# Shared rows in a table of their own, closing blocks that write one table, and a tail that reads one table

## The chip, the cores and the metric

The kernel runs on one core of a Trainium2 chip. The metric is the device time of one execution in microseconds (us): the median of 3 runs before the change is 1509.52 us (1507.58 to 1512.52). All data are fp32.

## The reference, cut to what matters

One layer over 1024 prompt tokens and 8 sample tokens, D = 1024. First a mixer (projection, convolution, retention, output projection), which leaves `x` (called x2 in the kernel) and the normed rows `h`. Then the part that the change touches:

```python
h = rmsnorm(x, g_ffn) * (1 + sc_f) + sh_f
x = x + gt_f * moe(h, ...)             # gt_f: one row for the prompt
# moe: 64 experts of width 256, top 6 per token
#   routed[t] = sum over 6 chosen experts of w * ((silu(h@w1[e]) * (h@w3[e])) @ w2[e])
#   shared    = (silu(h@ws1) * (h@ws3)) @ ws2
#   return routed + shared
y = x * rsqrt(mean(x*x) + eps) * g_final   # final RMSNorm
```

## The kernel before, in words

Up to about 712 us the mixer, the router and the sorting of tokens run. Then comes the **block stage**. Its unit is a block of 128 token slots; there are NX = 57 of them. The slots are dealt out in quarters of 32, so that a block serves one to three experts, in an order written out by a table (`GROUPS`, `LINE`, `QUARTERS`, lines 40 to 95). 64 experts x 3 MB of weights pass through five buffers, the ring (`SLOT`); expert s may be loaded into its slot when the block `FREE[s]` has finished with the former tenant: w1 and w3 after that block's up-product (`h_done`), w2 after its down-product (`y_done`). SP issues all these loads in order (`load_in_line`, lines 605 to 620, with L558 and L562 as the DMA lines).

Per block x:
- PE runs `up(x)` (L1017, 8 matmuls of 128x512 for a block with one expert), then `down(x-1)` (L1033, 4 matmuls), then `hidden_trans(x)` (L1023). `await_weights(x)` stands before `up`.
- ACT takes the SiLU (L1329), DVE the product (L1753), the scaling of the output by the routing weight (`blk_y`, L1764), the copy of the transposed hidden rows (L1757) and the transposes of gathered rows (`xpose`, L1744).
- POOL gathers block x+3 (L2005, 4 indirect DMAs) and then adds the scaled rows of block x into a DRAM table (`scatter`, L2014, an accumulating indirect DMA). A scatter waits for the one before it. Two tables lie behind each other in `acc_rows`; an expert's place in the line decides which of them it writes (even or odd), so both are complete only after the last scatters.

The shared expert is worked off beside this: `sh_down(n)` (L776) runs for 9 tiles of tokens, one in every fourth block from block 8 on (`SHARED_AT`). DVE multiplies each by gt_f (L1731), adds x2 (L1733), and ACT's DMA queue stores the sum back over x2 (`store_shared`, L1278) after it has loaded the old rows (`load_x2`, L1274).

**The tail** begins when both chains of scatters have landed (SP waits at lines 655 to 657). SP has loaded g_final and the 8 tiles of x2 beforehand (L646, L648). It now loads 3 small sample pieces and, alternately, 8 tiles of each table (L663, L664). PE adds the two tables by products with the identity (L1126; tile 0 is added on DVE, L1931), DVE multiplies by gt_f (L1935) and adds x2 (L1938), ACT squares and takes the root (L1350, L1353), DVE scales (`finish`, L1919, L1920), SP stores (L667).

Where the order of work is set: each engine runs its own written list; only semaphores join them. SP's list counts most here, since all big loads are in it one behind the other.

Of the kernel before, what the change touches and what calls it, by code (L numbers as in the profile page):

```python
# [20 lines left out]
P = 128  # L21
# [52 lines left out]
GROUPS = even_order(groups())  # L74
# [6 lines left out]
NU = len(QUARTERS) // 4  # L81
assert NU % 2 == 1 and all(len({x for x, _ in QUARTERS[4 * u:4 * u + 4]}) < 3 for u in range(NU))
# [19 lines left out]
SHARED_AT = tuple(8 + 4 * n for n in range(NT))  # L102
# [27 lines left out]
def build(nc, t, out):  # L130
    with ExitStack() as ctx:
# [3 lines left out]
        def sem(name):  # L135
# [32 lines left out]
        x3_ready, fin_ssq, fin_std, dve_step, pool_step = (  # L168
            sem(n) for n in "x3_ready fin_ssq fin_std dve_step pool_step".split())
# [5 lines left out]
        acc_in = [win_in[0], win_in[1]] + [win_in[2 + i // 2] for i in range(TP - 2)]  # L175
        acc_there = [16 + 32, 16 + 32] + [16 + 64] * (TP - 2)
# [16 lines left out]
        sh_rows_s = scratch("sh_rows_s", (NS, D))  # L193
# [44 lines left out]
        acc_t = [W[:, WE + D * i:WE + D * i + D] for i in range(TP)]  # L238
        acc_s = W[:, WE + TP * D:WE + TP * D + SW]
        odd_t = [W[:, WE + (TP + 1 + i) * D:WE + (TP + 1 + i) * D + D] for i in range(TP)]  # L240
        odd_s = W[:, WE + TP * D + SW:WE + TP * D + 2 * SW]
        sh_s = W[:, WE + TP * D + 2 * SW:WE + TP * D + 3 * SW]
# [95 lines left out]
        sh_x2 = (gt_m, gret[:, :, :].rearrange("p v n -> p (v n)"))  # L338
# [26 lines left out]
        x2_t += [mods[:, 2, :], mods[:, 3, :]]  # L365
        x2_s, gt_s, g_s = (gret[:, 0, SW * x:SW * x + SW] for x in range(3))
# [39 lines left out]
        def _(sp):  # L406
# [217 lines left out]

            rounds = sp.value_load(rounds_i, min_val=0, max_val=ROUNDS)
# [17 lines left out]
            sp.wait_ge(x2_in, 16)  # L643
            for n in range(2):
                sp.wait_ge(sh_stored[n], 16 * ((NT + 1 - n) // 2))
            sp.dma_start(g_fin, everywhere(t["g_final"].rearrange("(a n) -> a n", a=1))).then_inc(x2_in, 16)  # L646
            for i in range(TP):
                sp.dma_start(x2_t[i], x2_rows[P * i:P * i + P, :]).then_inc(x2_in, 16)  # L648
# [27 lines left out]
        def _(pe):  # L676
# [418 lines left out]
            for x in range(1, NX):  # L1095
                await_weights(x)
                up(x, parts_of(x), x % 2)
                if x in SHARED_AT:
                    sh_down(SHARED_AT.index(x))
# [1028 lines left out]
```

## Time and profile before

| | |
|---|---|
| median of 3 runs | 1509.52 us |
| the profiled execution | 1507.41 us, its span 1505.6 us |
| mixer and routing | 0 to 712 us of the span |
| block stage | first up-product 746.55 us, last evacuation 1447.79 us |
| last scatters | issued at 1435.67, 1445.46 and 1451.77 us, the last landed by 1458.17 us |
| tail | from 1458.17 us to the end |
| PE busy over the span | 1357.6 us (90%) |
| bytes moved | 370.74 MB, mean 246 GB/s |

The times of instructions below count from the start of the span. Between the end of the last instruction and the device time of the same execution lie 1.8 us.

### The profile page before, as it was taken

The page shows a single profiled execution, that of the slowest core. Times are in us where ns is not written, and L with a number is a line of the kernel's source. Part 1 is how long each engine was busy: PE and PEld are TensorE (multiplying, and loading weights), DVE is VectorE, ACT ScalarE, POOL GpSimd, SP SyncE. Part 2 cuts the span into 40 slices and gives each one's busy share as a digit, 9 for nine tenths or more (in the row PEclk, how much of TensorE's full clock was granted, in tenths as well). Part 3 has the DMA queues.
Part 4 walks back from the last instruction along what each step waited for, and adds up shares of the span by engine and source line. Part 5 has one row for each costly group of instructions (what it writes and reads, how often), then busy time and mean ns, then how long its engine had stood idle before and what let it go on. Part 6 is the DMA issues. An engine that isn't in the chain of part 4 may idle for free.

```text
span 1505.6 us, 17406 instructions
## 1 busy us (share of the span) xinstructions
PE 1357.6 (90%) x5860; PEld 616.6 (41%) x5860; DVE 823.9 (55%) x2088; ACT 207.0 (14%) x347; POOL 438.8 (29%) x379
## 2 busy tenths in 40 slices
PE   4889999999989999899699989989989999879947
PEld 2344454545545554455343433433333333323313
DVE  1048686988988899987233333332433343332327
ACT  1121223223131313232000000000000000000003
POOL 0000120212111112224334434444444444453410
PEclk9899999999999999999899999999999999999978
DMA  9988212121121001812999999999999999999976
GB/s 322 334 316 306 107 56 87 42 101 59 70 90 40 33 28 51 251 38 74 357 383 379 366 372 341 392 379 334 377 365 374 372 374 365 346 377 353 371 206 262
DMA packets 96810, 370.74 MB, mean 246 GB/s; under 512 B 18493, under 2 KB 32801, under 8 KB 71967
## 3 DMA queue, kind: packets, MB, share of 16 engines
q1 hardware_dynamic: 73463, 310.40, 53.4%
q0 software_dynamic: 20944, 50.89, 13.1%
q10 hardware_dynamic: 2320, 8.42, 1.4%
q8 instruction: 43, 0.70, 0.2%
q14 instruction: 40, 0.33, 0.1%
HBM read 326.03 MB, written 64.30 MB: 259 GB/s over the span
## 4 chain that ended last, share of the span: by engine, by line
PE 31%; DMA 12%; issue 5%; DVE 2%; POOL 1%; SPq 0%; ACT 0%; POOLq 0%; ACTq 0%
PE U L1017 19%; PE R L1033 9%; DMA acc_rows<-W,kT 5%; DMA acc_rows<-xr,kT 5%; PE X L776 2%; DMA W<-h_rows,q_r 1%; PE T L1023 1%; DMA front<-h_rows,q_r 1%; DVE W L1920 1%; DVE W L1938 1%; DVE W L1935 1%; PE R L1126 0%; DMA W<-acc_rows 0%; POOL W L2005 0%; POOL front L2005 0%
## 5 line engine op out<-in xcount | busy, mean ns | idle before, releaser
L729 PE MATMUL U<-W,front 128*128 128x512 f32 x768 | 343.7, 602 | 1.2 <-issue 1.2
L1435 DVE SCALAR_TENSOR_TENSOR cv<-win,cw,cv 128x128 f32<-128x128 f32 x960 | 256.6, 346 | 1.4
L1017 PE MATMUL U<-W,cat 128*32 128x512 f32 (+2 forms) x848 | 211.9, 625 | 24.4 <-issue 15.9
L1017 PE MATMUL U<-W,front 128*32 128x512 f32 (+2 forms) x1056 | 202.7, 611 | 17.4 <-issue 17.4
L729 PEld LDWEIGHTS U<-W,front 128*128 128x128 f32 x768 | 145.0, 194 | 168.6 <-issue 168.6
L1033 PE MATMUL R<-W,glu 128*32 128x512 f32 (+2 forms) x952 | 207.9, 596 | 1.3 <-DVE glu L1757 1.3
L1744 DVE STREAM_TRANSPOSE front<-front 128x1024 f32<-128x1024 f32 x28 | 57.3, 2045 | 147.9 <-DMA front<-h_rows,q_r 147.9
L1017 PEld LDWEIGHTS U<-W,cat 128*32 128x32 f32 (+2 forms) x848 | 78.2, 147 | 137.2 <-issue 136.1
L2005 POOL DMA_INDIRECT W<-h_rows,q_r x116 | 117.2, 1010 | 48.6 <-issue 34.8
L1033 PEld LDWEIGHTS R<-W,glu 128*32 128x32 f32 (+2 forms) x952 | 71.2, 134 | 131.5 <-issue 130.0
L1744 DVE STREAM_TRANSPOSE cat<-W 128x1024 f32<-128x1024 f32 x29 | 59.2, 2041 | 118.8 <-DMA W<-h_rows,q_r 107.6
L1017 PEld LDWEIGHTS U<-W,front 128*32 128x32 f32 (+2 forms) x1056 | 70.4, 131 | 128.9 <-issue 127.3
L2005 POOL DMA_INDIRECT front<-h_rows,q_r x112 | 112.9, 1008 | 34.2 <-issue 34.2
L823 PE MATMUL R<-W,cat 128*128 128x512 f32 x256 | 114.7, 606 | 1.7 <-ACT cat L1258 1.7
L1329 ACT ACTIVATE sg<-U 128x256 f32<-128x256 f32 x57 | 21.8, 383 | 682.6 <-PE U L1017 682.6
L1969 POOL DMA_INDIRECT list_tab<-list_val,list_row x54 | 54.2, 1004 | 187.6 <-DVE list_row L1529 141.7
L1960 POOL TENSOR_TENSOR o_t<-o_t,gret 128x512 f32<-128x512 f32 x8 | 10.1, 1264 | 297.5 <-DVE o_t L1596 278.6
L2014 POOL DMA_INDIRECT acc_rows<-xr,kT x29 | 46.6, 1607 | 169.0 <-DMA acc_rows<-W,kT 116.3
L2014 POOL DMA_INDIRECT acc_rows<-W,kT x28 | 44.7, 1598 | 157.0 <-DMA acc_rows<-xr,kT 85.8
L823 PEld LDWEIGHTS R<-W,cat 128*128 128x128 f32 x256 | 49.1, 194 | 61.0 <-issue 59.1
L1764 DVE TENSOR_SCALAR W<-R,kT 128x1024 f32<-128x1024 f32 x28 | 35.9, 1283 | 63.2 <-PE R L1033 63.0
L1753 DVE TENSOR_TENSOR sg<-U,sg 128x256 f32<-128x256 f32 x57 | 22.8, 400 | 83.6 <-ACT sg L1329 83.6
(371 smaller groups left out, 1216.5 us busy)
## 6 DMA issues: line engine op xcount, KB each, us to landing
W<-in_w SPq DMA_DIRECT2D x192, 1024.0 KB, 18.4
W<-in_w_ada SPq DMA_DIRECT2D x24, 1024.0 KB, 8.6
W<-in_w_in SPq DMA_DIRECT2D x6, 2048.0 KB, 19.9
W<-acc_rows SPq DMA_DIRECT2D x16, 512.0 KB, 9.7
front<-in_x_prompt SPq DMA_DIRECT2D x8, 512.0 KB
W<-in_w_out SPq DMA_DIRECT2D x1, 4096.0 KB, 17.8
xr<-in_x_prompt SPq DMA_DIRECT2D x8, 512.0 KB, 4.2
x_rows<-xr SPq DMA_DIRECT2D x8, 512.0 KB, 3.3
```

The lines of the kernel that those rows point to most:

```text
L729: last = mm(U[BANK[g]][:, :], hT[:, k, :], w_in[:, k, 512 * g:512 * g + 512], start=k == 0, stop=k == KT - 1)
L776: last = mm(X[0:rows, 512 * half:512 * half + 512], sh_hidT[g][f][:, at:at + rows], sh_w2[:, f, 512 * half:512 * half + 512], start=f == 0 ...
L823: last = mm(R[:, 512 * n:512 * n + 512], cat[:, k, :], w_out[:, k, 512 * n:512 * n + 512], start=start and k == ks[0], stop=stop and k == ...
L1017: last = mm(U[1][cols, :], xgT[z][:, k, cols], w13[:, :, k, :], start=k == 0, stop=k == KT - 1)
L1033: last = mm(R[cols, 512 * half:512 * half + 512], hidT[:, f, cols], weights[:, at:at + 512], start=f == 0, stop=f == FT - 1)
L1435: ins = v.scalar_tensor_tensor(cv[:, c, :], win[:, c, w:w + P], cw[:, c, w:w + 1], cv[:, c, :], ALU.mult, ALU.add)
L1744: v.transpose(xgT[z][:, :, :].rearrange("p k (q t) -> p k q t", q=4), xgs[r].rearrange("p (q t k) -> p k q t", q=4, k=KT)).then_inc(xgT_re ...
L1753: v.tensor_tensor(hid, U[1][:, DE:2 * DE], hsil, ALU.mult).then_inc(hid_ready, 1)
L1764: v.tensor_scalar(y_sbs[x % 2], R[:, :], slot_w[:, x:x + 1], None, ALU.mult).then_inc(y_evac, 1)
L1969: pool.indirect_dma_start(list_tab, bass.IndirectOffsetOnAxis(ap=list_row[0:rows, k:k + 1], axis=0), list_val[0:rows, k, :], None, bounds_ ...
L2005: pool.indirect_dma_start(xgs[x % 2][:, QW * q:QW * q + QW], None, h2_quarters, bass.IndirectOffsetOnAxis(ap=at[:, q, :], axis=0), bounds_ ...
L2014: pool.indirect_dma_start(acc_rows, bass.IndirectOffsetOnAxis(ap=at, axis=0), y_sbs[x % 2], None, bounds_check=2 * TABLE - 1, oob_is_err=F ...
```

## The change

Four things are changed, in one step.

1. **Shared rows.** `shared_out(n)` on ACT copies the product of `sh_down(n)` from PSUM and stores it to a DRAM table `shared_rows`. DVE's `sh_add` and the loads of x2 within the stage are gone; x2 stays as it was. Tiles 0 to 2 are done before the first block, the other six in every sixth block from block 8 on.
2. **The order of blocks.** Three groups with one expert and one block each (`CLOSING`) are taken out of the evenly spread order and put at the end. Their experts write the first table, so that the second is complete after block `ODD_LAST` = 53.
3. **Base rows.** For each of 8 tiles PE adds the shared rows and the odd table's rows (`base(i)`), and DVE multiplies by gt_f and adds x2 (`base_add(i)`), in place in `x2_t[i]`. `base(0)` stands between `up(56)` and `down(55)`, `base(1)` between `hidden_trans(56)` and `down(56)`, the others behind `down(56)`.
4. **Tail.** 8 tiles of one table are loaded. DVE multiplies by gt_f (`gate`), PE adds the base rows by the identity into PSUM, ACT and DVE read the sum from PSUM.

How the table of blocks changes (block: the experts by place in line whose weights it is the first to need; then, in brackets, the `FREE` block of each):

```
before   49: 55 56 [44 46]   50: 57 [46]   52: 58 59 [48 48]   53: 60 [49]   55: 61 [51]   56: 62 63 [52 52]
after    46: 54 55 [41 43]   47: 56 [43]   48: 57 [45]   49: 58 [46]   51: 59 [46]   53: 60 [48]   54: 61 [48]   55: 62 [50]   56: 63 [53]
```

The core of the diff:

```diff
+CLOSING = [x for x in MADE if len(x) == 1 and units_of(x) == 1][-3:]
+GROUPS = even_order([x for x in MADE if x not in CLOSING]) + CLOSING
+TABLE_OF = tuple(i % 2 for group in GROUPS for i in range(len(group)))
+END = [max(LAST[s] for s in range(NE) if SLOT[s] == r) for r in range(RING + 1)]   # 56 55 53 54 45
-SHARED_AT = tuple(8 + 4 * n for n in range(NT))
+SHARED_AT = (-1, -1, -1) + tuple(8 + 6 * n for n in range(NT - 3))
+        odd_in = [c_in] * 6 + [modv_in] * 2
+        odd_there = [48 + 96] * 6 + [80 + 32] * 2
+        shared_in = [sconv_in] * 2 + [disp_in] * 6
+        shared_there = [48 + 32] * 2 + [32 + 96] * 6
@@ sync, behind the last load_in_line
+            sp.wait_ge(y_done, END[RING] + 1)
+            for i in range(TP):
+                sp.dma_start(x2_t[i], x2_rows[P * i:P * i + P, :]).then_inc(x2_in, 16)
+            sp.dma_start(g_fin, ...).then_inc(x2_in, 16)
+            for i in range(2):
+                load_shared_rows(i)
+            sp.wait_ge(y_done, END[2] + 1)
+            sp.wait_ge(scattered[ODD_LAST % 2], 16 * (ODD_LAST // 2 + 1))
+            for i in range(6):
+                load_odd(i)
+            sp.wait_ge(xgT_ready, NX)
+            load_odd(6)
+            sp.wait_ge(h_done, NX - 1)
+            load_odd(7)
+            sp.wait_ge(y_done, END[3] + 1)
+            for i in range(2, TP):
+                load_shared_rows(i)
...
             for i in range(TP):
                 sp.dma_start(acc_t[i], ...).then_inc(acc_in[i], 16)
-                sp.dma_start(odd_t[i], ...).then_inc(acc_in[i], 16)
@@ tensor
+            sh_down(0)                       # ahead of spread_lists(); 1 and 2 ahead of up(0)
+            def base(i):
+                pe.wait_ge(shared_in[i], shared_there[i])
+                pe.wait_ge(odd_in[i], odd_there[i])
+                pe.wait_ge(base_ready, floor(i - 1))
+                for half in range(2):
+                    cols = slice(512 * half, 512 * half + 512)
+                    mm(base_banks[i % 2][half], ident[:, :], shared_t[i][:, cols], start=True, stop=False)
+                    last = mm(base_banks[i % 2][half], ident[:, :], odd_t[i][:, cols], start=False, stop=True)
+                last.then_inc(base_posed, 1)
-            for i in range(1, TP):
-                pe.wait_ge(acc_in[i], acc_there[i])
-                pe.wait_ge(gated, floor(i - 1))
+            for i in range(TP):
+                pe.wait_ge(gated, i + 1)
+                pe.wait_ge(base_ready, TP if i == 1 else i + 1)
+                pe.wait_ge(fin_ready, floor(i - 1))
                 for half in (slice(0, 512), slice(512, 1024)):
...
+                    mm((R, X)[i % 2][:, half], ident[:, :], acc_t[i][:, half], start=True, stop=False)
+                    last = mm((R, X)[i % 2][:, half], ident[:, :], x2_t[i][:, half], start=False, stop=True)
@@ scalar
+            def shared_out(n):
+                act.wait_ge(sh_downs, n + 1)
+                act.wait_ge(sh_stored[n % 2], 16 * (n // 2))
+                nc.scalar.activation(sh_y[n % 2][0:sh_rows(n), :], X[0:sh_rows(n), :], ACT.Copy).then_inc(sh_copied, 1)
+                act.wait_ge(sh_copied, n + 1)
+                act.dma_start(shared_rows[...], sh_y[n % 2][...]).then_inc(sh_stored[n % 2], 16)
@@ vector
+            def base_add(i):                 # even tiles: the same in four halves
+                    link(v.tensor_tensor(X[:, :], X[:, :], gt_f, ALU.mult))
+                    v.tensor_tensor(x2_t[i], X[:, :], x2_t[i], ALU.add).then_inc(base_ready, 1)
+            base_add(0)
             blk_y(NX - 1)
+            for i in range(1, TP):
+                base_add(i)
+            def gate(i):
+                dve.wait_ge(acc_in[i], acc_there[i])
+                v.tensor_tensor(acc_t[i], acc_t[i], gt_f, ALU.mult).then_inc(gated, 1)
+            for i in range(2, TP):
+                gate(i)
+                finish(i - 2)
```

How PE's list ends. Before, from the transpose of block 55 on (`sg` holds the hidden rows, `glu` the transposed ones, `U` and `R` are PSUM banks):

```order
L1023 MATMUL T<-ident,sg 128x128
L1017 MATMUL U<-W,cat 64x512 [waits xgT_ready,ring_in3,ring_in0]
L1017 MATMUL U<-W,cat 64x512 x15
L1033 MATMUL R<-W,glu 64x512 [waits y_evac,hidT_ready]
L1033 MATMUL R<-W,glu 64x512 x7
L1023 MATMUL T<-ident,sg 128x128 [waits hid_ready]
L1023 MATMUL T<-ident,sg 128x128
L1033 MATMUL R<-W,glu 64x512 [waits y_evac,hidT_ready]
L1033 MATMUL R<-W,glu 64x512 x7
```

After, the same place, from the down-product of block 55 on (`mods` and `W` hold the shared and the odd rows):

```order
L1134 MATMUL R<-W,ident 128x512
L1064 MATMUL R<-W,glu 128x512 [waits y_evac,hidT_ready]
L1064 MATMUL R<-W,glu 128x512 x3
L1054 MATMUL T<-ident,sg 128x128 [waits hid_ready]
L1054 MATMUL T<-ident,sg 128x128
L1133 MATMUL X<-mods,ident 128x512 [waits base_ready,c_in,sconv_in]
L1134 MATMUL X<-W,ident 128x512
L1133 MATMUL X<-mods,ident 128x512
L1134 MATMUL X<-W,ident 128x512
L1064 MATMUL R<-W,glu 128x512 [waits y_evac,hidT_ready]
L1064 MATMUL R<-W,glu 128x512 x3
L1133 MATMUL U<-W,ident 128x512 [waits base_ready,c_in,disp_in]
```

The first row is the last of `base(0)`'s four matmuls, which stand ahead of the down-product of block 55; `base(1)`'s four stand between the transpose and the down-product of block 56, and `base(2)` begins behind it.

SP's list behind the last expert's weights, before (`in_w` are expert weights, `x_rows` is x2):

```order
L558 DMA W<-in_w 128x2048 x2
L562 DMA W<-in_w 128x2048 [waits y_done]
L625 TENSOR_LOAD k_r
L646 DMA mods<-in_g_final 128x1024 [waits sh_stored1,sh_stored0,x2_in]
L648 DMA W<-x_rows 128x1024 x6
L648 DMA mods<-x_rows 128x1024 x2
```

and after:

```order
L568 DMA W<-in_w 128x2048 x2
L572 DMA W<-in_w 128x2048 [waits y_done]
L640 DMA W<-x_rows 128x1024 [waits sh_stored1,y_done,sh_stored0,x2_in]
L640 DMA W<-x_rows 128x1024 x5
L641 DMA mods<-in_g_final 128x1024
L644 DMA mods<-shared_rows 128x1024 x2
L647 DMA W<-acc_rows 128x1024 [waits scattered1,y_done]
L647 DMA W<-acc_rows 128x1024 x5
L647 DMA front<-acc_rows 128x1024 [waits xgT_ready]
L647 DMA front<-acc_rows 128x1024 [waits h_done]
L644 DMA W<-shared_rows 128x1024 [waits y_done]
L644 DMA W<-shared_rows 128x1024 x5
```

Between the last weights and the tail, 24 tiles of 512 KB (x2, odd and shared rows) stand where 8 stood; the odd table's eight were in the tail before, and no list read the shared rows of the prompt.

## Rows read from the trace of the kernel before

**Rows 1.** Stages: us, busy time by engine, PEclk, DMA share, GB/s.
```profile
core 0: us, PE busy (x) PEld busy (x) DVE busy (x) ACT busy (x) POOL busy (x), PEclk, DMA share, GB/s
800.00:900.00 100.00, 94.53 (x422) 36.94 (x423) 33.90 (x34) 3.06 (x8) 45.12 (x40) 0.98 1.01 373
...
1440.00:1460.00 20.00, 6.45 (x30) 1.95 (x26) 2.90 (x3) 0.00 (x0) 3.10 (x2) 0.82 0.45 78
1460.00:1480.00 20.00, 12.57 (x24) 5.60 (x25) 10.42 (x13) 4.52 (x9) 0.00 (x0) 0.67 1.00 389
```

**Rows 2.** PE's longest wait in the block stage: waits from 720 to 1440 us.
```profile
PE U L1017 <- issue: 33.3, 6, 8.1
```

**Rows 3.** The chain of waits, 1340 to 1365 us: start, us, what.
```profile
1345.54 8.10 issue
1353.64 8.85 PE U L1017 x32
```

**Rows 4.** The chain of waits over the stage: one `sh_down`.
```profile
946.87 3.43 PE X L776 x8
```

**Rows 5.** ACT's SiLU of blocks 50 and 51: the pace of the last eight blocks.
```profile
1373.27 0.38 ACT L1329 ACTIVATE sg<-U 128x256 f32<-128x256 f32 x1 [10.36 <-PE U L1017]
1384.16 0.38 ACT L1329 ACTIVATE sg<-U 128x256 f32<-128x256 f32 x1 [10.50 <-PE U L1017]
...
1438.98 0.38 ACT L1329 ACTIVATE sg<-U 128x256 f32<-128x256 f32 x1 [11.20 <-PE U L1017]
```

**Rows 6.** DMA queues, 1200 to 1300 us (packets, MB, share): q1 SP's, q10 ACT's.
```profile
q1 hardware_dynamic: 3765, 27.40, 67.6%
...
q10 hardware_dynamic: 160, 0.56, 1.4%
```

**Rows 7.** DMA queues and landing times, 1416 to 1440 us.
```profile
q1 hardware_dynamic: 1912, 7.20, 75.2%
...
W<-x_rows SPq DMA_DIRECT2D x6, 512.0 KB, 16.8
```

**Rows 8.** PE ahead of the first block, 718 to 757 us.
```profile
728.17 0.64 PE L1051 MATMUL U<-ident,k_d 128*32 128x128 f32 x2 [5.79 <-DMA k_d<-list_tab,v_t]
...
734.29 3.72 PE L765 MATMUL T<-front,W 128*128 128x264 f32 x16
746.55 8.65 PE L1017 MATMUL U<-W,cat 128*128 128x512 f32 x16 [8.54 <-DVE cat L1744]
```

**Rows 9.** POOL's scatter of block 54 and DVE's evacuation of block 56.
```profile
1435.67 1.58 POOL L2014 DMA_INDIRECT acc_rows<-xr,kT  x1 [8.46 <-DMA acc_rows<-W,kT]
...
1447.79 1.28 DVE L1764 TENSOR_SCALAR xr<-R,kT 128x1024 f32<-128x1024 f32 x1 [3.76 <-PE R L1033]
```

**Rows 10.** DMA landing times in us, 1450 to 1460 us.
```profile
W<-acc_rows SPq DMA_DIRECT2D x2, 512.0 KB, 4.4
W<-acc_rows SPq DMA_DIRECT2D x2, 32.0 KB, 1.7
```

**Rows 11.** The tail: PE's identity sums, ACT, DVE and SP, by start.
```profile
1458.17 0.35 SPq L659 DMA_DIRECT2D W<-acc_rows  x1
...
1467.43 6.58 PE L1126 MATMUL R<-W,ident 128*128 128x512 f32 x8 [19.69 <-DMA W<-acc_rows]
...
1487.81 3.60 PE L1126 MATMUL X<-W,ident 128*128 128x512 f32 x8
...
1491.24 3.60 PE L1126 MATMUL R<-W,ident 128*128 128x512 f32 x8
...
1496.78 1.22 DVE L1935 TENSOR_TENSOR W<-R,mods 128x1024 f32<-128x1024 f32 x1
1498.03 1.23 DVE L1938 TENSOR_TENSOR W<-W,mods 128x1024 f32<-128x1024 f32 x1
1499.35 1.06 ACT L1350 ACTIVATE sig<-W 128x1024 bf16<-128x1024 f32 x1 [2.31 <-DVE W L1938]
...
1501.06 1.28 DVE L1920 SCALAR_TENSOR_TENSOR W<-W,sm,mods 128x1024 f32<-128x1024 f32 x1
```

More of the change, by code:

```diff
@@ L237, in build @@
         x2_t = [shw[:, D * i:D * i + D] for i in range(6)]
[L238 to L242, printed above, removed]
+        odd_t = [W[:, WE + D * i:WE + D * i + D] for i in range(6)]
+        acc_t = [W[:, 4 * WE + D * i:4 * WE + D * i + D] for i in range(6)] + [W[:, 2 * WE + D * i:2 * WE + D * i + D] for i in range(2)]
+        acc_s, odd_s, sh_s = (W[:, 2 * WE + 2 * D + SW * i:2 * WE + 2 * D + SW * i + SW] for i in range(3))
+        shared_t = [W[:, 3 * WE + D * i:3 * WE + D * i + D] for i in range(6)]
         ident = sb("ident", [P, P])
@@ L364, in build @@
         gt_f, g_fin = mods[:, 0, :], mods[:, 1, :]
-        x2_t += [mods[:, 2, :], mods[:, 3, :]]
-        x2_s, gt_s, g_s = (gret[:, 0, SW * x:SW * x + SW] for x in range(3))
+        x2_t += sh_y
+        odd_t += [x_t[:, :], front[:, D:2 * D]]
+        shared_t = [mods[:, 3, :], mods[:, 4, :]] + shared_t
+        x2_s, gt_s, g_s = (maskT[:, x, 0:SW] for x in range(1, 4))
         same_row = maskT[:, 0, :]
@@ L641, in _ @@
                         load_expert(e, 0)
[L643 to L648, printed above, removed]
-            sp.dma_start(same_row, t["same_row"]).then_inc(sample_in, 16)
-            sp.dma_start(x2_s, in_pieces(x2_rows[SEQ:TOKENS, :])).then_inc(sample_in, 16)
-            for b in range(NS):
-                rows = slice(b * P // NS, (b + 1) * P // NS)
-                sp.dma_start(gt_s[rows], in_pieces(mod_rows[1 + b:2 + b, 5 * D:6 * D])).then_inc(sample_in, 16)
-                sp.dma_start(g_s[rows], t["g_final"].rearrange("(c n) -> c n", n=SW)).then_inc(sample_in, 16)
             sp.wait_ge(scattered[0], 16 * EVEN + 16 * NE * rounds)
@@ L1073, in _ @@
             sh_up_part(2, 1, 1)
+            sh_down(1)
+            sh_down(2)
             def parts_of(x):
@@ L1099, in _ @@
                     sh_down(SHARED_AT.index(x))
+                if x == NX - 1:
+                    base(0)
                 down(x - 1, parts_of(x - 1))
                 hidden_trans(x)
+                if x == NX - 1:
+                    base(1)
                 if x == 3:
@@ L1105, in _ @@
             down(NX - 1, parts_of(NX - 1))
+            for i in range(2, TP):
+                base(i)
             ring_0 = [(0, 4, ring[0])]
@@ L1318, in _ @@
             score(TP - 1)
-            for g in (1, 2):
-                sh_silu_part(g, 0)
-                sh_silu_part(g, 1)
-            act.wait_ge(x2_stored, 16 * TP)
-            for n in range(2):
-                load_x2(n)
+            sh_silu_part(1, 0)
+            sh_silu_part(1, 1)
+            sh_silu_part(2, 0)
+            shared_out(0)
+            sh_silu_part(2, 1)
+            shared_out(1)
+            shared_out(2)
             def blk_silu(n):
@@ L1927, in _ @@
             v.tensor_tensor(acc_s, acc_s, x2_s, ALU.add).then_inc(x3s_ready, 1)
-            for i in range(TP):
-                if i == 0:
-                    dve.wait_ge(acc_in[i], acc_there[i])
-                    link(v.tensor_tensor(acc_t[i], acc_t[i], odd_t[i], ALU.add))
-                    ins = v.tensor_tensor(acc_t[i], acc_t[i], gt_f, ALU.mult)
-                else:
-                    dve.wait_ge(sum_done, i)
-                    ins = v.tensor_tensor(acc_t[i], (X, R)[i % 2][:, :], gt_f, ALU.mult)
-                ins.then_inc(gated, 1)
-                dve.wait_ge(gated, i + 1)
-                v.tensor_tensor(acc_t[i], acc_t[i], x2_t[i], ALU.add).then_inc(x3_ready, 1)
-                if i > 0:
-                    finish(i - 1)
+            for i in range(2, TP):
+                gate(i)
+                finish(i - 2)
+            finish(TP - 2)
             finish(TP - 1)
```

85 lines of the change are left out of this document (44 added, 41 removed).

## The prediction, written before the changed kernel was run

> **What bounds the kernel now.** I read the stages first, then PE's waits, then the chain of waits, the DMA queues, and last the tail in order of time. The stages show the two halves of the question. In the block stage the DMA engines are busy all the time (share 1.01) while PE is busy 94.5%; in the tail the DMA share falls and TensorE's clock with it [rows 1]. PE's waits in the block stage are 6 in number and 33.3 us in sum, all at an up-product and with "issue" as the releaser [rows 2], which the kernel's code explains: `await_weights` stands there. The chain shows the last of them: PE waits 8.10 us for the weights of block 49, and then runs the rest of the stage without one [rows 3]. So up to block 49 the stage goes at the pace at which weights arrive, and from there at PE's pace, 10.9 us for a block [rows 5]. After it come the last scatters; the one of block 54 begins at 1435.67 us, that of 56 waits for its evacuation at 1447.79 us and for 55's landing [rows 9]; the tail starts at 1458.17 us [rows 11]. In the tail PE's sum of two tiles takes 3.60 us by its row and 3.43 from one start to the next (1487.81 to 1491.24), the first one 6.58 us at the lower of the two clocks, and DVE spends 1.22 + 1.23 + 1.28 = 3.7 us per tile and a short reciprocal [rows 11]: DVE bounds the tail.
>
> **The block stage.** The weights' bytes are the same, 3.15 MB for each expert. What changes is what goes beside them and by when they are needed.
> - *Bytes gone.* In the stage, six loads of x2 and eight stores of full tiles (0.52 MB each) become five stores: 9 x 0.524 = 4.7 MB less. SP's and ACT's queues together moved 27.40 + 0.56 = 28.0 MB in 100 us [rows 6], SP's alone 7.20 MB in 24 us [rows 7], so 0.28 to 0.30 MB per us; I take 0.29. That is 16.2 us of weights' time. The three early stores take the place of two early loads of x2, 0.52 MB more at a time when the queues are full: +1.3 us.
> - *Need moved forward.* By the tables of blocks, block 49 waited for the 57th expert of the line (place 56). In the new order the last place where the demand is as dense is block 46, which needs the 56th (place 55): one expert fewer, 3.15 / 0.29 = 10.8 us earlier. These weights then land at 1353.6 - 16.2 + 1.3 - 10.8 = 1327.9 us. But behind block 46 stand 11 blocks, not 8. Before, from the end of the wait to the evacuation of block 56 it was 1447.8 - 1353.6 = 94.2 us for 8 blocks [rows 3, 9]; three more at 10.9 us [rows 5] make 126.9. The evacuation of block 56 would thus come at 1454.8 us, **7 us later** than now, although 4.7 MB fewer are moved. The closing blocks need a whole expert each, but their loads are issued three blocks ahead and I see no wait there.
> - *What is free.* `sh_down` costs PE 3.43 us [rows 4]. Three of them leave the stage, which gives nothing while PE waits for weights anyway, and stand before it: number 0 fits in the wait of 5.79 us at 728.17, numbers 1 and 2 (6.9 us and a copy of about 1.1 between, by ACT's row of 1.06 for the same elements [rows 11]) in the 8.54 us ahead of the first up-product [rows 8]. If that cover failed, it would cost 2 to 3 us, which the weights' pace would take up. DVE loses 8 x 2.4 us of work beside PE, ACT gains 9 copies of about a microsecond: neither bounds the stage.
>
> **The wait of `base(0)`.** It stands ahead of `down(55)`, so behind it on PE are the down-products of blocks 55 and 56, and behind those two scatters. Its semaphore counts all six first tiles of the odd table. Those are issued when block 53's scatter has landed, 1435.67 us before [rows 9], 1442.7 with the 7 us. In SP's queue they stand behind 1.05 MB of weights, 4.19 of x2, 0.52 of g_final and 1.05 of shared rows, all issued from the end of `down(53)` on (about 1427): 6.81 MB at the 7.20 MB in 24 us of such a stretch [rows 7], 0.30 MB per us, is 22.7 us, up to 1449.7. The six tiles, 3.15 MB at the tail's 389 GB/s [rows 1], since POOL has one scatter left to move, take 8.1 us, and the landing about 1.7 [rows 10]: 1459.5 us. `up(56)` ends at 1438.98 + 7.1 = 1446.1 [rows 5]. **PE waits 13.4 us.** From both sides: 0 if the odd tiles came without a queue before them, 20 if POOL's traffic ran beside them all the time. PE then begins at the lower clock. After 19.69 us of idling, the mean granted clock being 0.82 in its first 20 us and 0.67 in the next [rows 1], the same four matmuls took 6.58 us [rows 11]; I take 6.6 (3.4 if the clock stayed).
>
> The Trainium skill (DMA: Bandwidth & Descriptors, "Queues, rings and completion order") says that each DMA engine consumes a queue's descriptors in ring order. The trace fits: the x2 tiles, issued behind weights, landed 16.8 us after issue [rows 7]. By that page's limit of about 358 GB/s from HBM (section "Specifications") the six tiles would take 8.8 us, 0.7 more; the tail's 389 GB/s [rows 1] is above it, and the measurement decides.
>
> **PE's work behind the blocks.** `base(i)` is the same work as the tail's sums: 4 matmuls of 128x512 with the identity. `base(0)` 6.6 and `base(1)` 3.4 us delay `down(56)`: evacuation at 1454.8 + 13.4 + 6.6 + 3.4 = 1478.2. `base(2)` to `base(7)`: 6 x 3.43 = 20.6, to 1498.8. DVE's `base_add` (2.45 us for an odd tile by the rows of 1.22 and 1.23, four halves of 0.7 for an even one by estimate from these) keeps up with 3.43; only the last is added: 2.45. Then `gate(0)`, 1.23, which stands behind it on DVE: 1502.5. Block 56's scatter, issued about 1480, has landed by 1487 and the 8 tiles of 0.52 MB (10.8 us at 389 GB/s) by 1500: hidden.
>
> **The tail.** PE bounds it: 8 sums x 3.43 = 27.4 us, where 7 sums ran beside DVE before. A sum waits for the finish two tiles earlier; from SQUARE's start to the end of the scaling it is 1501.06 + 1.28 - 1499.35 = 2.99 us [rows 11], under 3.43. These two now read PSUM; an evacuation of that size from PSUM takes 1.28 [rows 9], the same as the scaling from SBUF, so I add nothing (between nothing and 0.4 per tile, which the gap to 3.43 covers). To 1529.9. Last square to scaling 3.0: 1532.9. From the last scaling to the span's end it was 1505.6 - 1502.3 = 3.3: **span 1536.2**, 30.6 more. The loads taken out of the tail (4.2 MB) give nothing, as DVE was its bound. The profiled execution took 1507.4 at a span of 1505.6; with the same 1.8 the new one takes 1538.0. The median lies 2.1 above the profiled run; I forecast 1540.
>
> **Rivals.**
> - *A: the odd tiles are in time and `base(0)` does not wait.* For it: 0.52 MB loads land in 4.4 us where the queue is empty [rows 10]. Against: 6.8 MB stand before them. Then 13.4 + 3.2 us fall away: 1536.2 - 16.6 = 1519.6 of span, 1523 as a median.
> - *B (the other side): the stage gets its 16 us.* If the last wait for weights stayed 8 blocks from the end, the freed bytes would bring the evacuation of block 56 to 1447.8 - 16.2 + 1.3 = 1432.9; and if `base(0)` doesn't wait either, the rest is 6.9 (two bases) + 20.6 + 2.45 + 1.23 + 27.4 + 6.3 = 64.9: span 1497.8, median 1502. It decides where the evacuation of block 56, without the bases, comes before 1505.6 - 64.9 = 1440.7, 7 us earlier than now. For it: PE's 33.3 us of waits are there to be won. Against: 11 blocks of PE's pace from block 46 on.
> - *C: the order costs the stage nothing (evacuation at 1447.8), but `base(0)` waits as forecast:* 1529 of span, 1533. Its result lies in the forecast's own spread.
> - *D: more waits.* The closing blocks take 3.15 MB in each 10.9 us, and block 56's w2 is issued only after `down(53)`; if it comes late, PE waits 3 to 10 us more at block 56 (the base tiles then come nearer to that, so about half is kept): 1543 to 1546.
>
> **How the numbers follow.** Forecast with C and D as its spread 0.76 (1530 to 1552), A 0.15, B 0.06, something else 0.03. The range that leaves out two in ten at most: 1518 to 1550. What a measurement of this kernel can tell from no change is 0.3%, 4.5 us. Slower by more: 0.90, within: 0.04, faster: 0.06.
>
> **What would show it.** In the new trace: the last "issue" wait of PE ahead of an up-product at block 46 (wrong if at 49 or later, then the stage's sum fails); a wait of 10 to 17 us at the first identity product with the odd rows as releaser, and that product at 6.6 us (wrong: A); six identity products without a gap behind the last down-product; tail products of 3.4 us in an unbroken row with DVE waiting for PE, and no row of tail loads in the chain. A span under 1515 would refute the sum as a whole.

## The result, and the profile after

The changed kernel takes 1547.83 us (median of 4 runs, 1545.36 to 1550.95) against 1510.05 us of the kernel before on the same chip: a ratio of 1.0245, 95% interval 1.0216 to 1.0275, 37.8 us slower. The forecast was 1540, in a range of 1518 to 1550. The profiled execution took 1545.5 us with a span of 1543.6.

The waits of PE from 720 us to the end (us in sum, times, longest) answer to [rows 2]:
```profile
PE U L1048 <- issue: 45.2, 8, 8.5
PE U L1133 <- issue: 14.2, 1, 14.2
PE R L1177 <- DVE W L1976: 7.8, 1, 7.8
```
The waits for weights grew from 33.3 to 45.2 us. Three more follow: 14.2 us ahead of the first identity product, and 7.8 us and, further on, 1.06 us in the tail, where PE stood idle for 19.69 us before [rows 11].

The chain of waits of the changed kernel (start, us, what) answers to [rows 3]:
```profile
1319.59 8.49 issue
1328.09 9.17 PE U L1048 x32
...
1434.37 18.62 DMA mods<-shared_rows
1452.99 7.76 issue
1460.75 2.05 PE U L1133 x2
...
1498.58 1.24 DVE X L1936
1505.05 1.24 DVE W L1976
...
1512.98 1.28 ACT L1402
```
The last wait for weights ends at 1328.09 us. Then nothing is late until the base tiles. The chain passes through the shared rows' loads, which land at 1452.99; the 7.76 us from there to 1460.75 have no releaser in this trace. The odd rows' loads are the ones behind them in SP's list, and a later kernel names them at the same product. Between the last `base_add` and the first gate the chain has a hole.

The stages, in the columns of [rows 1]:
```profile
1440.00:1460.00 20.00, 6.55 (x16) 2.61 (x14) 1.53 (x3) 0.39 (x1) 1.58 (x1) 0.79 1.03 386
1460.00:1480.00 20.00, 19.25 (x41) 8.70 (x42) 6.75 (x9) 0.00 (x0) 2.17 (x2) 0.86 0.63 209
1480.00:1500.00 20.00, 18.12 (x42) 7.52 (x40) 14.94 (x19) 0.00 (x0) 0.93 (x1) 1.00 0.72 235
1500.00:1520.00 20.00, 12.61 (x25) 5.42 (x26) 10.45 (x14) 4.46 (x9) 0.00 (x0) 0.83 0.09 38
```
From 1440 to 1460 us the DMA engines are full (1.03; before 0.45) and PE is idle for two thirds of the time. From 1500 to 1520 nothing is bound by DMA (0.09), and PE is busy for 12.61 us of 20 only.

The end in order of time, all engines, answers to [rows 5, 9, 11]:
```profile
1446.59 0.39 ACT L1382 ACTIVATE sg<-U 128x256 f32<-128x256 f32 x1 [10.14 <-PE U L1048]
1460.75 2.05 PE L1133 MATMUL U<-mods,ident 128*128 128x512 f32 x2 [14.20 <-issue]
1477.32 1.28 DVE L1801 TENSOR_SCALAR xr<-R,kT 128x1024 f32<-128x1024 f32 x1 [2.96 <-PE R L1064]
1499.85 1.22 DVE L1937 TENSOR_TENSOR gret<-X,gret 128x1024 f32<-128x1024 f32 x1
1505.05 2.36 DVE L1976 TENSOR_TENSOR W<-W,mods 128x1024 f32<-128x1024 f32 x2 [3.98 <-issue]
1506.33 2.08 PE L1177 MATMUL R<-W,ident 128*128 128x512 f32 x2 [7.79 <-DVE W L1976]
1512.98 1.28 ACT L1402 ACT_TABLE_LOAD   x1
1516.23 1.10 PE L1177 MATMUL R<-W,ident 128*128 128x512 f32 x2 [1.06 <-DVE W L1972]
1539.08 1.28 DVE L1972 SCALAR_TENSOR_TENSOR W<-X,sm,mods 128x1024 f32<-128x1024 f32 x1
```
Block 56 has its up-product at 1446.59 us but is evacuated at 1477.32, because PE stands before `base(0)`. The last `base_add` ends at 1501.07 and the first gate starts at 1505.05. For these 3.98 us DVE is idle, and the profile names no other engine or transfer that it waited for ("issue").

### The profile page after: what moved, and what is told of

Read it like the earlier page. It is cut to its first block, busy times and chain, and to the rows that moved or that the text cites. A ratio compares the mean times of both kernels' runs of the same rounds, so it can differ in the third digit from the quotient of the medians.

```text
span 1543.6 us, 17575 instructions
## 1 busy us (share of the span) xinstructions
PE 1398.4 (91%) x5932; PEld 634.2 (41%) x5932; DVE 814.2 (53%) x2086; ACT 216.6 (14%) x356; POOL 438.8 (28%) x379
## 4 chain that ended last, share of the span: by engine, by line
PE 48%; DVE 19%; DMA 16%; issue 9%; SPq 4%; ACT 2%; POOL 2%; DVEq 0%; POOLq 0%; ACTq 0%
PE U L1048 15%; DVE cv L1484 8%; PE R L1064 8%; PE U L760 7%; PE R L854 6%; DMA acc_rows<-W,kT 5%; DMA acc_rows<-xr,kT 4%; PE X L807 2%; DMA W<-h_rows,q_r 2%; SPq L448 2%; DMA W<-in_w_ada 2%; DMA front<-h_rows,q_r 1%; PE X L796 1%; DMA mods<-shared_rows 1%; PE R L724 1%
## 5 line engine op out<-in xcount | busy, mean ns | idle before, releaser
L2062 POOL DMA_INDIRECT acc_rows<-W,kT x28 | 44.7, 1598 | 189.6 <-DVE W L1801 119.1
```

Source lines behind the costliest of these rows:

```text
L2062: pool.indirect_dma_start(acc_rows, bass.IndirectOffsetOnAxis(ap=at, axis=0), y_sbs[x % 2], None, bounds_check=2 * TABLE - 1, oob_is_err=F ...
```

## The experiments

Each result stands beside the kernel before, run on the same chip. Two kernels, the first part of the change as a whole and the one with the loops moved, ran on another chip than the rest; the kernel before took 1511.02 us there and 1509.99 on the first. The ratios and their intervals are estimates from all the runs of both kernels, not quotients of the two medians. The experiments go from the block stage to the end.

### The order alone
```
--- the kernel before
-GROUPS = even_order(groups())
+MADE = groups()
+CLOSING = [x for x in MADE if len(x) == 1 and units_of(x) == 1][-3:]
+GROUPS = even_order([x for x in MADE if x not in CLOSING]) + CLOSING
```


> The kernel before with the changed order of blocks alone (closing groups at the end); tables, shared rows and tail as before. My theory: the last wait for weights moves from block 49 to about block 46, and 11 blocks at 10.9 us stand behind it instead of 8, less 10.8 us for one expert fewer: +22 us, 1532. Rival: PE's 33 us of waits are slack that the order only deals out anew: within 5 us of before, 1510.

Measured: 1529.75 us (1527.81 to 1530.74), ratio 1.0117 (1.0086 to 1.0147), 19.7 us slower. The theory holds (1532 forecast), and its rival (1510) falls: the evacuation of block 56 comes at 1469.42, 21.6 us later than before. PE's up-products that waited for weights, of this kernel, the fourth, sixth and last of eight:
```profile
996.19 8.43 PE L1019 MATMUL U<-W,front 128*32 128x512 f32 x64 [6.61 <-issue]
...
1141.78 9.02 PE L1019 MATMUL U<-W,cat 128*32 128x512 f32 x64 [11.73 <-issue]
...
1343.21 7.30 PE L1019 MATMUL U<-W,cat 128*64 128x512 f32 x24 [6.27 <-issue]
```
and the same three of the changed kernel:
```profile
988.23 8.41 PE L1048 MATMUL U<-W,front 128*32 128x512 f32 x64 [7.15 <-issue]
...
1127.23 8.88 PE L1048 MATMUL U<-W,cat 128*32 128x512 f32 x64 [8.32 <-issue]
...
1328.09 9.17 PE L1048 MATMUL U<-W,cat 128*64 128x512 f32 x32 [8.49 <-issue]
```
With the order alone the last wait ends at 1343.21, block 46, 10.4 us earlier than the 1353.6 of [rows 3], and three blocks more follow. That holds the prediction's second step. The first, the bytes, is the difference of the two fences: 8.0 us at the fourth wait, 14.6 at the sixth, 15.1 at the last (14.9 forecast, 16.2 less 1.3). This difference holds more than bytes: with them three `sh_down` left the stage, 10.3 us of PE's work, and no run takes the two apart in the new order.

### The bytes alone, in the old order
First without the loads of x2 in the stage:
```
--- the kernel before
-            for n in range(2):
-                load_x2(n)
...
-                    load_x2(n + 2)
...
-                v.tensor_tensor(sh_x2[n % 2], X[:, :], sh_x2[n % 2], ALU.add).then_inc(sh_copied, 1)
+                v.tensor_copy(sh_x2[n % 2], X[:, :]).then_inc(sh_copied, 1)
```


> The kernel before, but the eight loads of x2 in the block stage are left out, and the shared expert's rows are stored (as bytes, after the multiplication by gt_f) to a table that nobody reads; the shared part is missing in the output. Order and tail as before. My theory: the stage up to block 49 goes at the pace of bytes, 4.2 MB fewer at 0.29 MB per us are 14.5 us: 1495. Rival: the weights' landing is set by slots coming free, not by bytes: 1508 to 1510.

Measured: 1501.87 us (1496.32 to 1503.89), ratio 0.9929 (0.99 to 0.9958), 8.1 us faster: between the theory (1495) and its rival (1508 to 1510). Then the first part of the change as a whole, which keeps the output:
```
--- the kernel before
+SHARED_AT = (-1, -1, -1) + tuple(8 + 6 * n for n in range(NT - 3))
...
+            for i in range(TP):
+                if i >= 4:
+                    sp.wait_ge(base_ready, i - 3)
+                sp.dma_start(x2_t[i], x2_rows[P * i:P * i + P, :]).then_inc(ada_in[i % 4], 16)
...
+                    sp.dma_start(part, shared_rows[P * i:P * i + P, wide * z:wide * z + wide]).then_inc(stage_in[i % 4], 16)
...
+                    ins = v.tensor_tensor(part, part, gt_f[:, wide * z:wide * z + wide], ALU.mult)
...
+                    ins = v.tensor_tensor(to, part, to, ALU.add)
```


> Part 1 of the change alone, in the old order of blocks: shared rows stored plainly by ACT, tiles 0 to 2 ahead of the blocks. x2 and shared rows (not the odd table) are loaded behind the last weights through four staging buffers, DVE alone makes x2 + gt_f * shared (tile 0 in block 55, tile 1 in block 56, the others behind the last evacuation), no sum on PE but the old tail's. Theory 1: bytes and the three down-products that leave the stage both count, as between the run with the order alone and the changed kernel (last wait for weights ends at 1343.2 and 1328.1): here it ends at 1338.5 instead of 1353.6, the last evacuation at 1433; the extra loads beside the last scatters give back 3 to 8 us, so 1498 to 1502. Theory 2: only the loads' bytes count, 8 us as in the run without x2 loads: last wait ends at 1345, and with the same contention no gain at all, 1505 to 1510.

Measured: 1509.42 us (12 runs) against 1511.02, ratio 0.9986 (0.9967 to 1.0005): no difference. That is what theory 2 said (last wait ends at 1345, 1505 to 1510); theory 1 falls. The chain of waits of the kernel without the loads of x2:
```profile
1337.21 7.91 issue
1345.12 9.29 PE U L1018 x32
```
and of the one with the first part whole:
```profile
1336.87 8.00 issue
1344.87 9.36 PE U L1026 x32
```
Both end the last wait 8.5 to 8.8 us earlier than before, whether 4.2 MB or the whole first part's bytes are gone. By bytes at 0.29 MB per us it would have been 14.5 and about 15. One observation narrows the cause: the w2 of the expert at place 56 was issued 8.3 us earlier without the loads (1325.95 against 1334.27 us), and PE's wait ended about 19 us behind that issue in both. Ahead of it SP issued nothing for 13.3 us in either kernel (from 1320.92 before). So in the old order the last weights are held back by the slot that PE must free first, and not only by the bytes before them. Why the first part as a whole is worth 15.1 us in the new order and 8.8 in the old one stays open. PE stands idle for longer in the new order (51.8 us with the order alone against 33.3), so there is more to be won; that this is the reason isn't shown.

Part one gained 8.6 us up to the evacuation of block 56 (1439.23, [rows 9]: 1447.79) and ended where it began. POOL and SP of this kernel show where it went:
```profile
1448.04 2.48 POOL L2028 DMA_INDIRECT acc_rows<-xr,kT  x1 [8.75 <-DMA acc_rows<-W,kT]
...
1455.03 0.42 SPq L645 DMA_DIRECT2D maskT<-in_g_final  x1
...
1460.23 0.35 SPq L668 DMA_DIRECT2D W<-acc_rows  x1
```
From the last scatter to the tail's first load it is 12.2 us here, against 6.4 before (1451.77 to 1458.17). But only 7.4 of them are the scatter, which has landed at 1455.4. SP is what comes last: it issues its small loads until 1455.45, and for the next 4.8 us the trace shows no instruction of it. By the program these are its own reading of the number of extra rounds and its own empty loop over them. In the kernel before that loop stood ahead of the loads of g_final and x2, where SP shows a like gap (1411.88 to 1416.55) long before the tail. The change moved these loads ahead of the loop, and so the loop to the end. The same 4.8 us stand behind the small loads in five of the kernels below, however early the last scatter has landed.

### The base sums out of the way of the last blocks
```
--- the changed kernel
-                if x == NX - 1:
-                    base(0)
...
-                if x == NX - 1:
-                    base(1)
...
-            for i in range(2, TP):
+            for i in range(TP):
                 base(i)
...
-            base_add(0)
             blk_y(NX - 1)
-            for i in range(1, TP):
+            for i in range(TP):
                 base_add(i)
```


> The changed kernel with base(0) and base(1) moved behind the last down-product, and their adds behind the last evacuation on DVE. My theory: the evacuation of block 56 comes at 1454 instead of 1477, but the first base sum still starts when the odd tiles land (1461), so 8 sums end at about 1491.6 instead of 1498.4: 7 us of the 24 come back, 1541. Rival: the whole delay of the down-products was on the path: 1524.

Measured: 1545.59 us (1538.44 to 1548.75), ratio 1.0208 (1.0165 to 1.0251): 2.2 us less than the changed kernel, too little to tell apart. The rival (1524) falls; the theory's 1541 is missed by 4.6. The evacuation of block 56 came at 1456.45, 21 us earlier, and the last scatter was issued at 1462.80 instead of 1479.38. PE of this kernel:
```profile
1464.48 2.04 PE L1133 MATMUL U<-mods,ident 128*128 128x512 f32 x2 [8.07 <-issue]
...
1477.03 1.91 PE L1133 MATMUL U<-W,ident 128*128 128x512 f32 x2 [2.50 <-DMA W<-shared_rows]
```
So the 21 us by which the last block's evacuation and scatter are delayed cost nothing: the eight sums form a chain from the landing of the odd rows to the first gate, and the last scatters fit beside it. What should have come back is the 7.1 us of the two down-products, which in the changed kernel stand in that chain between the sums. It was lost again in three places. PE gets the odd rows 3.7 us later, 1.0 of it because this stage ran that much later (scatter 54 at 1442.62 against 1441.60); the rest fits the scatter of block 55, which now runs beside them. It waits 2.5 us for the shared rows of tile 2, which was hidden before. And after that wait the sum of tile 2 takes 5.2 us instead of 3.4. The last `base_add` starts at 1500.90, 1.05 us later than in the changed kernel.

### The base sums left out, with and without their loads
```
--- the changed kernel
-            for i in range(2, TP):
-                base(i)
...
-                pe.wait_ge(base_ready, TP if i == 1 else i + 1)
...
-            for i in range(1, TP):
-                base_add(i)
```


> The changed kernel without the base sums and their adds (odd and shared rows are loaded but left out of the output). My theory: evacuation of block 56 at 1454, last scatter landed about 1468 beside the loads, first gate 1474, first sum at the lower clock, then 3.43 us each: span 1512, median 1517. So the base sums with their place and wait cost 31 us of the 38. Rival: the new tail by itself (PE's sums in series with the finishes) is slower than the old one, 1525 or more.

Measured: 1522.79 us (1520.69 to 1525.02), ratio 1.0074 (1.0052 to 1.0096): between the theory (1517) and its rival (1525 or more). The sums with their place and wait cost 25.0 us and not 31. And with the loads gone too:
```
--- the kernel above
-            for i in range(2):
-                load_shared_rows(i)
...
-            for i in range(6):
-                load_odd(i)
...
-            load_odd(6)
...
-            load_odd(7)
...
-            for i in range(2, TP):
-                load_shared_rows(i)
```


> The changed kernel without its sums of odd and shared rows, and now without the 16 loads of these rows either (both parts are missing in the output). With the loads but without the sums it took 1522.8 us, and there the scatters of blocks 55 and 56 took 10.5 and 13.3 us from issue to what waited for them, against 5.5 and 6.3 before. Theory (the 8.4 MB of loads beside them slow the scatters): evacuation of block 56 stays near 1454.5, the two scatters take 5 to 7 us each, the tail's first load is issued at 1465 to 1467 instead of 1475.4, and the median is 1513 to 1515. Rival (an accumulating scatter takes its 10 to 13 us whatever runs beside it, or waits for something of the new order): the first load stays near 1475, the median at 1521 to 1524.

Measured: 1511.46 us (10 runs), ratio 1.001 (0.9992 to 1.0027). POOL and SP of the kernel with the loads:
```profile
1451.64 1.55 POOL L2055 DMA_INDIRECT acc_rows<-W,kT  x1 [9.43 <-DMA acc_rows<-xr,kT]
1462.16 1.55 POOL L2055 DMA_INDIRECT acc_rows<-xr,kT  x1 [8.97 <-DMA acc_rows<-W,kT]
...
1470.23 0.42 SPq L667 DMA_DIRECT2D maskT<-in_g_final  x1
1475.43 0.35 SPq L691 DMA_DIRECT2D W<-acc_rows  x1
```
and without them:
```profile
1452.35 1.55 POOL L2047 DMA_INDIRECT acc_rows<-W,kT  x1 [8.90 <-DVE W L1788]
1459.32 1.55 POOL L2047 DMA_INDIRECT acc_rows<-xr,kT  x1 [5.42 <-DMA acc_rows<-W,kT]
...
1448.50 0.42 SPq L659 DMA_DIRECT2D maskT<-in_g_final  x1
1465.38 0.35 SPq L683 DMA_DIRECT2D W<-acc_rows  x1
```
The 8.4 MB that nobody waits for in either kernel cost 11.3 us, and the tail's first load comes 10.05 us later with them. The rival, that the scatters are slow by themselves, falls. The theory's first load (1465 to 1467) came at 1465.38 and its median is 1.5 us off, but slower scatters are only a part of what the loads cost. I had taken the 13.3 us from the last scatter to the first load for the scatter's time. Beside the loads the last two scatters landed 9.7 and 9.0 us after their issue, without them 6.1 and 5.9: the last has landed at 1471.2 and 1465.2 us, so this explains 6.0 of the 10.05. The other 4.2 are SP's own. Beside the big loads its small ones are issued until 1470.65 (without them until 1448.92), and then come the same 4.8 us without an instruction of SP, up to 1475.43. Without the big loads SP has passed that loop long before and waits for the scatter alone. Over 1440 to 1460 us the DMA engines moved 364 GB/s at a share of 1.02 in the first, and 182 GB/s at 0.63 in the second.

The Trainium skill (DMA: Bandwidth & Descriptors, "Queues, rings and completion order") says that each DMA engine takes turns between the queues it has work for, a packet at a time. The slowdown of the landings from 6.1 to 9.7 and from 5.9 to 9.0 us when a second queue is full agrees with it in kind; no run shows the turns themselves.

### The loops over extra rounds ahead of the base sums
```
--- the kernel with late base sums, DVE (and so on PE, with base(i))
-            for i in range(TP):
-                base_add(i)

             dve.wait_ge(rounds_known, 1)
             rounds = dve.value_load(rounds_i, min_val=0, max_val=ROUNDS)
             with dve.Fori(0, ROUNDS) as rd:
...
+            for i in range(TP):
+                base_add(i)
```


> The changed kernel with all base sums behind the last down-product and, on PE and DVE, behind the loop over extra rounds (which runs no round here), so that this loop is passed while PE waits for the odd rows instead of between the last base add and the first gate. Theory: DVE's 4.0 us between the last base add and the first gate fall away, and with it most of PE's idle time, so its clock stays high: 4 to 6 us off the 1545.6 of the kernel with late base sums alone, 1540. Rival: the 4 us are a wait for the acc tiles, which land then: no change, 1545.

Measured: 1540.42 us (1539.67 to 1545.08), ratio 1.0204 (1.0168 to 1.024). DVE of this kernel goes from the last `base_add` to the gates without the gap of 3.98 us:
```profile
1498.15 1.22 DVE L1933 TENSOR_TENSOR gret<-X,gret 128x1024 f32<-128x1024 f32 x1
1499.29 2.35 DVE L1972 TENSOR_TENSOR W<-W,mods 128x1024 f32<-128x1024 f32 x2
```
The trace bears out the first half of the theory. The kernel with late base sums had the gap too, 3.98 us up to its gate at 1506.10, though its acc tiles' loads were all issued by 1483.60 and landed 7.1 us after issue in the median; so the rival, a wait for these tiles, falls. The gap is the time in which DVE reads the count of extra rounds, which is none, and passes the skipped bodies. Before, this loop stood where DVE was idle for 11.82 us anyway, waiting for the tail's data (1449.07 to 1460.89).

The second half fails. PE's idle time ahead of the first gated sum fell from 7.78 to 3.72 us, but that sum took 5.24 us all the same:
```profile
1500.56 1.13 PE L1173 MATMUL R<-W,ident 128*128 128x512 f32 x2 [3.72 <-DVE W L1972]
```
Nor do the times resolve the gain: the medians lie 5.2 us apart, but on two chips, and the ratios to the kernel before, 1.0208 and 1.0204, are the same within their intervals. Of the 7.0 us between the two profiled spans (1544.9 and 1537.9), 4.1 are the gap; 2.8 were there already at the first base sum (1464.48 and 1461.69).

### All but the order
```
--- the kernel above
-GROUPS = even_order([x for x in MADE if x not in CLOSING]) + CLOSING
+GROUPS = even_order(list(MADE))
```


> The changed kernel with its blocks in the old order; as the last scatter into the odd table is then block 56's, its 8 sums of odd and shared rows stand behind the last down-product and behind the loop over extra rounds. The same with the new order took 1540.4 us. The order by itself cost 19.7 us in the kernel before. Theory (the sums form a chain that starts where the odd tiles land, so what the order costs the stage is hidden behind that wait): evacuation of block 56 at about 1439, 17 us earlier than 1456.45, its scatter landed at about 1460, the six odd tiles at about 1470, sums to 1501, first gate ends 1504.5, span 1538, median 1538 to 1542, no faster than with the new order. Rival (the costs of the order and of the sums add up): 19.7 us less, 1520 to 1523.

Measured: 1534.06 us (1532.07 to 1535.5), ratio 1.0162 (1.0133 to 1.0191): 6.4 us less than with the new order, 5.3 if each is taken against the kernel before on its own chip; the profiled spans are 5.4 apart. PE and POOL of this kernel:
```profile
1443.70 1.55 POOL L2058 DMA_INDIRECT acc_rows<-xr,kT  x1 [4.81 <-DMA acc_rows<-W,kT]
...
1460.43 2.04 PE L1133 MATMUL U<-mods,ident 128*128 128x512 f32 x2 [21.36 <-DMA W<-acc_rows]
...
1470.67 1.13 PE L1133 MATMUL U<-W,ident 128*128 128x512 f32 x2 [0.61 <-DMA W<-shared_rows]
```
and the first and third base sum with the new order:
```profile
1461.69 2.05 PE L1133 MATMUL U<-mods,ident 128*128 128x512 f32 x2 [7.85 <-DMA W<-acc_rows]
...
1474.28 1.91 PE L1133 MATMUL U<-W,ident 128*128 128x512 f32 x2 [2.52 <-DMA W<-shared_rows]
```
Both name the odd rows (`acc_rows`) as what released the first base sum. Neither theory has its number, but the first is the nearer. The order costs this stage 14.8 us (block 56 is evacuated at 1439.12 against 1453.89), of which `base(0)` sees 1.3 (1460.43 against 1461.69). The other 4 us of the difference arise within the sums: PE waits 0.61 us for the shared rows of tile 2 instead of 2.52, and the sum after that wait is faster. The last two scatters, with almost nothing beside them (SP's queue moved 0.08 MB from 1437 to 1450 us), took 6.4 and 6.2 us, so that the last landed at 1449.9 and not at my 1460, and with it the odd tiles ten microseconds before my 1470. The late release of the odd table, for which the new order was there, costs nearly nothing: with block 56 itself writing it, the sums begin no later.

### A version that is not slower
```
--- the kernel of the first part
-                if x >= NX - 2:
-                    base_add(x - NX + 2)
+                if x >= NX - 2:
+                    base_add(2 * (x - NX + 2))
+                    base_add(2 * (x - NX + 2) + 1)
...
-            for i in range(2, TP):
+            for i in range(4, TP):
```


> The kernel of the first part alone (shared rows stored plainly, x2 + gt_f * shared by DVE in four staging buffers, old order, old tail, 1509.4 us) with DVE's first four sums one block earlier, so that the loads of tiles 4 to 7, which wait for them, leave the time of the last two scatters. Theory (the last block's scatter took 12.2 us beside these loads against 6.3 before, and that ate the 8.6 us gained in the block stage): loads of tiles 6 and 7 issued at about 1435 instead of 1443 to 1446, last scatter 8 to 10 us, the tail's first load at 1456 to 1458 instead of 1460.2, median 1505 to 1507. Rival (the same bytes are moved in any case, so they only trade places with the scatter of block 55): 1508 to 1511.

Measured: 1505.20 us (12 runs), ratio 0.9978 (0.9961 to 0.9996); profiled span 1500.9. POOL and SP:
```profile
1444.76 2.51 POOL L2029 DMA_INDIRECT acc_rows<-xr,kT  x1 [6.00 <-DMA acc_rows<-W,kT]
...
1449.48 0.42 SPq L645 DMA_DIRECT2D maskT<-in_g_final  x1
1454.73 0.35 SPq L668 DMA_DIRECT2D W<-acc_rows  x1
```
The median has the theory's number, and the tail begins 5.5 us earlier than in the first part alone, but not for the theory's reason. The scatter is no faster: it landed 7.3 us after its issue (7.4 there). It was issued 3.3 us earlier, and SP, which is again what comes last, was through with its small loads at 1449.90 instead of 1455.45; the empty loop of 4.8 us follows in both. No run moves that loop away from the end. The median is 42.6 us below the changed kernel's; against the kernel before it is 0.22% faster (0.04 to 0.39%): the sign is just resolved, the size is not. Nor is the step from the first part alone (ratio 0.9986, 0.9967 to 1.0005) resolved by the times.

## Why the prediction was right, and where it was short

The measured 1547.8 us lies within the range, near its upper end, 7.8 above the forecast. Up to the last base sum the path that I had told is right within about a microsecond; the tail was short.

**The block stage: right in its times.** The last wait for weights ends at 1328.09, forecast 1327.9, at block 46. The need (10.4 us, forecast 10.8) was measured by itself. The bytes (15.1, forecast 14.9) were measured together with the three `sh_down` that left. Eleven blocks at PE's pace then lead to an evacuation of block 56, in the four kernels of the new order without the base sums in its way, at 1453.9 to 1456.5; forecast 1454.8. The price of 0.29 MB per us is no constant: in the old order the same part of the change was worth 8.8 us. Rival B priced a stage in the old order by it, at a gain of 14.9 us, and was wrong by 6 of them; had the change kept the old order, my forecast of its stage would have been too early by as much. So the price came out right here, and it is partly luck that it did. The 1.3 us for the three early stores is also too small by my own price (0.52 / 0.29 = 1.8).

**The wait of `base(0)`: right, with two errors that cancel.** 14.2 us from 1446.55 to 1460.75, forecast 13.4 from 1446.1 to 1459.5; its products took 5.8 us, forecast 6.6. The evacuation of block 56 followed at 1477.32, forecast 1478.2. But the loads ahead of the odd rows had landed at 1452.99 and not at 1449.7, and the odd rows followed 7.8 us later and not 9.8. The sign I had named, the odd rows as the releaser, this trace doesn't give ("issue"); the kernels with the loops moved give it.

**What I had said of this wait was only half of it.** I told it by what stands behind it on PE. The late base sums show that the 21 us by which the last evacuation is delayed cost nothing: the path runs through the odd rows, the eight sums with the two down-products between them, and the first gate, and the last scatters fit beside it.

**The base sums: right.** Six with one gap of 0.4 us, the last `base_add` ended at 1501.07, forecast 1501.25.

**The tail: short by 7.4 us.** This is the step that failed, in two terms. "Then `gate(0)`, 1.23, which stands behind it on DVE": between the two stands the loop over extra rounds, 4.0 us, so the gate ended at 1506.28 and not at 1502.5. I had priced only what the profile counts as busy. And "8 sums x 3.43 = 27.4": they took 31.0, from 1506.28 to 1537.3. PE had been idle for 7.79 us, and the first sum, its first four pairs of products, took from 1506.33 to 1511.58, 5.25 us (1.8 more than 3.43, PEclk 0.83 in that stage). The table load of 1.28 us ahead of the first square root stands in the chain to the first finish, for which the third sum waits, and PE waited another 1.06 there. From the last sum to the end it was 3.1 and 3.2 us, as forecast. The forecast span of 1536.2 plus 3.8 for the gate and 3.6 for the sums is the measured 1543.6.

**A row read wrong.** I wrote that in the tail the DMA share falls. It is 0.45 from 1440 to 1460 us, but 1.00 from 1460 to 1480 [rows 1], and PE's 19.69 us of idling there end with a load. The tail with half the table loads, in the kernel without the base sums and their loads, took 44.7 us from its first load to the end of the span (1465.38 to 1510.1), against 47.4 before. So the lighter tail was worth 2.7 us and not nothing; in the changed kernel its earlier loads are hidden behind the base sums.

**The rivals.** A (no wait) and B are refuted by the 14.2 us and by block 46. C is refuted in the stage: without the base sums in its way block 56 is evacuated 6 to 9 us later than before. D came nearest with its time, 1543 to 1546, for a wrong reason: no wait for weights came after 1328 us in the blocks.

**Where 37.8 us come from.** The changed kernel without its sums and their loads takes 1511.5: order, bytes and a lighter tail nearly cancel. The loads add 11.3 (1522.8), by the traces about 6 through slower scatters and about 4 through SP's empty loop, which they push back. The sums with their wait add 25.0 (1547.8). Of these, 4.0 are DVE's empty loop by the trace. The order is worth 5 to 6 us at the end, though it costs the stage 14.8.

## What to carry to other kernels

A load that nobody waits for is not free while a serial chain of scatters runs: look at what else is in flight where the last transfers are, and at what the engine that issues these loads still has to do behind them. Where a new consumer needs data that exist only at the end, its whole work stands behind that landing, so price the chain from the landing and not the wait alone. And an empty loop on an engine is a cost as soon as it comes between two steps of the critical path: it has no row of its own, only an idle time without a releaser. Here it happened twice, on DVE and on SP. When a time "from issue to what waited for it" grows, first check that the one who waited was ready: the last instruction of that engine, and the landing time of the transfer itself, tell the two apart.

## What the runs showed of the hardware

- The last two accumulating scatters of 128 rows landed 5.5 to 6.3 us after their issue with few other transfers (the kernels before and changed, and the one without sums and loads), and 9.7 and 9.0 us beside a full SP queue (the one without the sums).
- One core's DMA engines moved 386 GB/s over the 20 us from 1440 of the changed kernel, and 406 GB/s in the last kernel's tail:
```profile
1460.00:1480.00 20.00, 15.96 (x35) 7.24 (x36) 14.09 (x15) 6.09 (x11) 0.00 (x0) 0.82 1.02 406
```
That is 13% above the limit of about 358 GB/s per core which the Trainium skill gives (DMA: Bandwidth & Descriptors, "Specifications"); its page Perfetto Trace Analysis ("Roofline") says that a core alone can pull more, up to about 435, and these rows agree with that.
- A loop of extra rounds that is never entered held DVE for 3.98 us in two kernels, and SP for 4.8 us in six.
- The first identity sum after an idle time of PE took longer than the 3.4 us of the others: 5.2 us after 3.7 us of idling (the kernel with the loops moved), 5.25 after 7.8 and 5.8 after 14.2 (the changed kernel, where PEclk was 0.83 from 1500 to 1520 us and 0.86 from 1460 to 1480).
